# A two-block hybrid model on one core: where early sums, biases, softmax scaling and modulation passes stand around the first output projection

## The chip, the cores and the metric

The kernel runs as one program on one core of a Trainium2 chip. The metric is the device time of one execution in microseconds. Three runs of the kernel before gave a median of 2509.61 us (2504.63 to 2519.35). A core has TensorE (PE, with its weight loads PEld), VectorE (DVE), ScalarE (ACT), GpSimd (POOL) and SyncE (SP), each with its own instruction stream; they meet at semaphores. SP issues the loads of weights, POOL those of the modulation weights.

## The reference

Two blocks follow each other on x of 256 tokens by 2048. The first is a mixer of attention (8 heads of 128) and a state space part (16 heads of 64) side by side, then a gated FFN with a convolution. What the change touches is the first block's mixer:

```python
mod = jax.nn.silu(c) @ w_ada[l] + b_ada[l]
shift_m, scale_m, gate_m, shift_f, scale_f, gate_f = jnp.split(mod[:, None, :], 6, axis=-1)
h = rms_norm(x, norm_mix_g[l]) * (1.0 + scale_m) + shift_m
proj = h @ w_in[l]
q, k, v, xs, z, bmat, cmat, dt_raw = jnp.split(proj, split_at, axis=-1)
attn = moba_attention(q.reshape(hd), k.reshape(hd), v.reshape(hd), rel_bias)
attn = rms_norm(attn, attn_norm_g[l])
ssm = ssd_mixer(xs, z, bmat, cmat, dt_raw, conv_w, conv_b, dt_bias, a_log, d_skip, norm_g)
mix = jnp.concatenate([attn, ssm], axis=-1) @ w_out[l]
x = x + gate_m * mix
h = rms_norm(x, norm_ffn_g[l]) * (1.0 + scale_f) + shift_f
x = x + gate_f * conv_ffn(h, w_up[l], conv_ffn_w[l], conv_ffn_b[l], w_down[l])
```

With 256 tokens there is one attention block: softmax(q k^T / sqrt(128) + bias by distance, causal) v. In the state space part, with dt = softplus(dt_raw + dt_bias) and cs the running sum of -exp(a_log) dt, head h gives y[l] = sum over s <= l of (C_l . B_s) exp(cs_l - cs_s) dt_s x_s, plus d_skip x, times silu(z), and a norm over each half of the width.

## The kernel before, in words

Everything is held transposed, channels on partitions and the 256 tokens in the free dimension. A weight matrix is streamed in units of 128 x 2048 fp32 (1 MB). SP loads a unit into one of four slots of w_raw (load_w, a slot is reloaded once TensorE has used it), ScalarE casts it to w_hi (`hi`, `hi_unit`), VectorE takes the rest w_lo = w_raw - w_hi (`lo`, `lo_unit`), and TensorE makes three matmuls for each product: hi by hi, hi by lo, lo by hi. h_both holds the normed activations, h_hi and h_lo, in the same split. `chunk` runs four units over four output tiles in four PSUM banks.

The modulation vector is worked out on VectorE beside all this: `ada(pair, slot)` multiplies a load of 128 x 2048 in one of two slots of ada_raw by c and sums it into one column of mod. POOL issues the load of a pair when the pass two before it is done. There are 192 passes in all, 2 x 96; those up to 63 are done before the first output projection, 64 to 79 in it, and each engine's stream is written out by hand, so the place of a pass in VectorE's order is fixed.

The stretch in question, in order:
- the input projection IN1 ends with the tokens' v. VectorE and ScalarE take it out of PSUM, cast and cut units 0 and 1 of OUT1;
- TensorE turns the dt and running-sum rows, makes C B^T and turns x (16 transposes); VectorE masks and makes x_tok in four products;
- SP has written the running sums to DRAM (cs_rows) and, once IN1's last unit is used, spreads them over the partitions into cs_b (four loads, in the place of h_hi). For each of 16 heads ScalarE forms the difference and the exponential in one of four buffers lm (L1314, L1325), VectorE multiplies by the masked C B^T (L1989), TensorE multiplies by x_tok (L549, L550), and VectorE adds it to xbc. Behind heads 2, 6, 10 and 14 stands an ada pass;
- VectorE multiplies by silu(z) (ssm_gated); ScalarE squares it, TensorE sums the squares with a matrix of ones (`stat`, L766);
- attention runs in two halves b of four heads: scores on TensorE, logits with bias on VectorE, exps on ScalarE with the row sums, reciprocals on VectorE, `scaled` (L1342) on ScalarE, transposes on TensorE (L988), `turned` and `attended` copies on ScalarE, the product with v (L994, L995);
- the attention output is squared, summed and normed, and OUT1 (U_OUT1, 16 units; L769 to L771) starts with its two state space units, then takes the two attention units. Its chunks end in add_to_x (L2041);
- mix_sq holds the squares of the first 12 tiles of x, VectorE reduces them to mix_sum (L2142), and with the last four tiles they give the norm ahead of the FFN's first half (UP1A, L774).

The bias tiles are loaded from a DRAM scratch in which POOL's bias row was put; the load of half 0 waits for the last state space output (ssm_y 8), since it lies where dt and lm lie, that of half 1 for ssm_gated 2.

## Time and profile before

| | |
|---|---|
| median of 3 runs | 2509.61 us (2504.63 to 2519.35) |
| profiled execution | 2508.57 us |
| its span in the profile | 2506.9 us |
| TensorE busy | 96% |
| VectorE busy | 75% |
| ScalarE busy | 46% |
| mean DMA rate | 245 GB/s |

The profile is of one execution. Times within it are microseconds from the start of its span. Matmuls are pipelined: the start of one row to the start of the next is what one costs, and the duration in a row overlaps its follower.

### The profile page before, as it was taken

To read this page: it belongs to the slowest core of one execution; us is meant where nothing else is said; L and a number is where in the kernel's file an instruction comes from. 1 tells how busy PE (TensorE), PEld (TensorE's weight loads), DVE (VectorE), ACT (ScalarE), POOL (GpSimd) and SP (SyncE) were. 2 spreads that over 40 slices of the span, in tenths; PEclk is the share of its full clock that TensorE was granted. 3 is DMA by queue.
4 is the path that set the end of the run, shared out by engine and by line. 5 is a ranking of instruction groups with operands and counts; after the bars stand their busy time and mean duration, and the time that the engine had idled before them with its cause. 6 is when DMAs were issued, how large, how long until landed. Compare 5 with 4: busy or idle time off the path is not lost.

```text
span 2506.9 us, 42171 instructions
## 1 busy us (share of the span) xinstructions
PE 2395.3 (96%) x17090; PEld 2130.7 (85%) x17090; DVE 1892.5 (75%) x2272; ACT 1142.3 (46%) x1288; POOL 87.8 (4%) x184
## 2 busy tenths in 40 slices
PE   8999959899999999999899999999999999999998
PEld 6799849888888888888799888888888888888887
DVE  6778879888887788887988677668888655566655
ACT  2144364455654345553544344433655543455442
POOL 0010001000000000000000000000000000000000
PEclk9999979899999999999999999899999999999999
DMA  9988948677787887778577123318776555555552
GB/s 398 420 339 331 339 166 315 259 295 288 269 302 296 336 322 278 277 266 326 224 296 305 69 92 117 106 63 300 270 271 238 187 189 185 185 188 196 186 220 100
DMA packets 88533, 614.75 MB, mean 245 GB/s; under 512 B 9657, under 2 KB 13393, under 8 KB 15057
## 3 DMA queue, kind: packets, MB, share of 16 engines
q1 hardware_dynamic: 65218, 444.03, 47.1%
q0 software_dynamic: 23184, 168.83, 17.8%
q8 instruction: 100, 1.64, 0.3%
q14 instruction: 31, 0.25, 0.0%
HBM read 608.60 MB, written 4.22 MB: 244 GB/s over the span
## 4 chain that ended last, share of the span: by engine, by line
PE 76%; DVE 11%; DMA 8%; ACT 3%; issue 2%; SPq 0%; DVEq 0%; POOLq 0%; ACTq 0%
PE ps L774 37%; PE ps L776 19%; PE ps L769 4%; PE ps L771 4%; PE ps L770 4%; DMA first_raw<-in_ada_stream 4%; DVE ada_raw L1748 2%; DMA ada_raw<-in_ada_stream 2%; DMA w_raw<-in_w_stream 1%; DVE w_lo L1736 1%; DVE w_lo L1732 1%; PE ps L655 1%; ACT w_hi L1174 1%; PE ps L816 1%; DVE xbc L1898 1%
## 5 line engine op out<-in xcount | busy, mean ns | idle before, releaser
L774 PE MATMUL ps<-h_both,w_hi 128*128 128x512 f32 x2816 | 987.1, 395 | 10.2 <-DVE h_both L1773 9.2
L776 PE MATMUL ps<-h_both,w_lo 128*128 128x256 f32 x2816 | 789.2, 280 | 0.0
L774 PEld LDWEIGHTS ps<-h_both,w_hi 128*128 128x128 f32 x2816 | 529.7, 188 | 135.3 <-issue 11.7
L1732 DVE TENSOR_TENSOR w_lo<-w_raw,w_hi 128x2048 fp32r<-128x2048 f32 x217 | 495.2, 2287 | 95.2 <-ACT w_hi L1168 88.1
L776 PEld LDWEIGHTS ps<-h_both,w_lo 128*128 128x128 f32 x2816 | 533.3, 189 | 0.0
L1168 ACT CAST w_hi<-w_raw 128x2048 fp32r<-128x2048 f32 x218 | 415.5, 1911 | 247.5 <-DMA w_raw<-in_w_stream 231.1
L774 PE MATMUL ps<-hid_both,w_hi 128*128 128x512 f32 x1344 | 471.7, 394 | 3.4 <-DVE w_lo L1736 3.4
L769 PE MATMUL ps<-h_both,w_hi 128*128 128x256 f32 x1408 | 406.7, 289 | 23.7 <-DVE h_both L1773 7.4
L1736 DVE TENSOR_TENSOR w_lo<-w_raw,w_hi 128x2048 fp32r<-128x2048 f32 x139 | 317.9, 2289 | 143.0 <-ACT w_hi L1174 140.8
L770 PE MATMUL ps<-h_both,w_hi 128*128 128x256 f32 x1408 | 399.6, 284 | 0.0
L771 PE MATMUL ps<-h_both,w_lo 128*128 128x256 f32 x1408 | 399.5, 284 | 0.0
L1174 ACT CAST w_hi<-w_raw 128x2048 fp32r<-128x2048 f32 x138 | 262.6, 1908 | 281.6 <-DMA w_raw<-in_w_stream 280.0
L1748 DVE SCALAR_TENSOR_TENSOR ada_raw<-ada_raw,ada_c 128x2048 f32<-128x2048 f32 x160 | 365.2, 2284 | 28.5 <-DMA ada_raw<-in_ada_stream 28.4
L776 PE MATMUL ps<-hid_both,w_lo 128*128 128x256 f32 x1344 | 375.1, 279 | 0.0
L774 PEld LDWEIGHTS ps<-hid_both,w_hi 128*128 128x128 f32 x1344 | 251.8, 187 | 64.8 <-issue 4.5
L769 PEld LDWEIGHTS ps<-h_both,w_hi 128*128 128x128 f32 x1408 | 271.2, 193 | 31.9 <-issue 13.0
L770 PEld LDWEIGHTS ps<-h_both,w_hi 128*128 128x128 f32 x1408 | 271.5, 193 | 0.3
L771 PEld LDWEIGHTS ps<-h_both,w_lo 128*128 128x128 f32 x1408 | 271.3, 193 | 0.0
L776 PEld LDWEIGHTS ps<-hid_both,w_lo 128*128 128x128 f32 x1344 | 251.9, 187 | 0.0
L2056 DVE SCALAR_TENSOR_TENSOR conv_y<-tmp,par,conv_y 128x254 f32<-128x254 f32 (+1 forms) x352 | 146.4, 478 | 5.1
L2335 POOL DMA_DIRECT2D ada_raw<-in_ada_stream x160 | 84.6, 529 | 1661.2 <-DVE ada_raw L1748 1628.4
L2049 DVE TENSOR_TENSOR tmp<-ps,tmp 128x1024 f32<-128x1024 f32 x44 | 53.9, 1224 | 113.3 <-ACT tmp L1380 113.3
(359 smaller groups left out, 2017.1 us busy)
## 6 DMA issues: line engine op xcount, KB each, us to landing
w_raw<-in_w_stream SPq DMA_DIRECT2D x364, 1024.0 KB, 4.9
ada_raw<-in_ada_stream POOLq DMA_DIRECT2D x160, 1024.0 KB, 6.5
first_raw<-in_ada_stream SPq DMA_DIRECT2D x32, 1024.0 KB, 12.6
w_more<-in_w_stream SPq DMA_DIRECT2D x8, 1024.0 KB, 14.9
kept_raw<-in_w_stream SPq DMA_DIRECT2D x4, 1024.0 KB, 8.1
x<-in_x_t SPq DMA_DIRECT2D x1, 2048.0 KB, 7.9
cs_b<-cs_rows SPq DMA_DIRECT2D x4, 512.0 KB, 7.5
x_kept<-x SPq DMA_DIRECT2D x1, 2048.0 KB, 14.8
```

The source lines that it names most:

```text
L769: mm(o, hi, r_hi, start=first, stop=False, **kw)
L770: mm(o, hi, r_lo, start=False, stop=False, **kw)
L771: return mm(o, lo, r_hi, start=False, stop=last, **kw)
L774: mm(ps[:, b, :].rearrange("p (a t) -> p a t", a=2), hi, both[:, :, k], start=first, stop=False, skip_group_check=True)
L776: return mm(ps[:, b, T:512], lo, big[:, k], start=False, stop=False, skip_group_check=True)
L1168: nc.scalar.copy(w_hi[:, slot], w_raw[:, slot]).then_inc(hi_ready, 1)
L1174: nc.scalar.copy(w_hi[:, u % 4], w_raw[:, u % 4]).then_inc(hi_ready, 1)
L1732: tt(w_lo[:, slot], w_raw[:, slot], w_hi[:, slot].bitcast(F32), ALU.subtract).then_inc(lo_ready, 1)
L1736: tt(w_lo[:, u % 4], w_raw[:, u % 4], w_hi[:, u % 4].bitcast(F32), ALU.subtract).then_inc(lo_ready, 1)
L1748: stt(out=rows, in0=rows, scalar=1.0, in1=ada_c[:], op0=ALU.mult, op1=ALU.mult, accum_out=col(mod, pair)).then_inc(ada_done, 1)
L2056: last = stt(out=conv_y[:, par_, i, d:T], in0=tmp[:, i, 0:T - d], scalar=pc(par_name, o + 2 - d), in1=conv_y[:, par_, i, d:T], op0=ALU.mul ...
L2335: G.dma_start(ada_raw[:, slot], src).then_inc(ada_loaded[slot], 16)
```

## The change

The cs_b load of the first four heads goes to tmp, and is issued ahead of the end of IN1; the bias tiles lie in tiles 8 to 15 of h_lo and are loaded right behind cs_b. x_tok is made and awaited in two halves. w_lo and w_hi of OUT1's unit 1 are made later, those of units 2 and 3 at other places. `scaled(0)` and `turned(0)` move from ScalarE to VectorE. The PSUM banks of the two halves of attention are exchanged, so that OUT1's first unit can run once half 0 is copied out; the sums for the attention norm come behind that unit. The ada passes 60 to 63 are placed differently, 64 to 75 run ahead of the cuts of chunks 1 to 3 of OUT1, and 76 to 79 behind the last of them. Context lines are cut.

```diff
@@ -209,6 +209,9 @@
             prob_t_a = sb(under, "prob_t", [P, 4, 384])
+        with ExitStack() as under:
+            sb(under, "before_bias", [P, 24, T])
+            bias = [sb(under, f"bias{b}", [P, 4, T]) for b in range(2)]
         h_both = sb(ctx, "h_both", [P, 2, KT, T], F32R)
@@ -243,7 +246,7 @@
                 sb(under, "xbc_heads", [P, HT, T])
-                bias_b = sb(under, "bias_b", [P, 4, T])
+                sb(under, "xbc_pairs", [P, 4, T])
                 logit_b = sb(under, "logit_b", [P, 4, 384])
@@ -253,7 +256,7 @@
             with ExitStack() as t:
-                bias = [sb(t, "bias", [P, 4, T]), bias_b]
+                sb(t, "dt_room", [P, 4, T])
                 logit = [sb(t, "logit", [P, 4, 384]), logit_b]
@@ -460,20 +463,17 @@
+            src = bass.AP(tensor=cs_rows, offset=0, ap=[[0, P], [T, 4], [1, T]])
+            sp.dma_start(tmp[:], src).then_inc(side_loaded[0], 16)
+            sp.wait_ge(bias_built, 1)
+            sp.dma_start(scratch.ap(), bias_row[:]).then_inc(bias_out, 16)
+            sp.wait_ge(bias_out, 16)
             sp.wait_ge(units_used, U_OUT1 + 2)
-            for q in range(4):
+            for q in range(1, 4):
                 src = bass.AP(tensor=cs_rows, offset=4 * q * T, ap=[[0, P], [T, 4], [1, T]])
...
             units(U_OUT1 + 3, U_OUT1 + 4)
-
-            sp.wait_ge(bias_built, 1)
-            sp.dma_start(scratch.ap(), bias_row[:]).then_inc(bias_out, 16)
-            sp.wait_ge(bias_out, 16)
             for b in range(2):
-                if b:
-                    sp.wait_ge(S("ssm_gated"), 2)
-                else:
-                    sp.wait_ge(S("ssm_y"), 8)
                 src = bass.AP(tensor=scratch, offset=b * 4 * 384, ap=[[1, P], [384, 4], [1, T]])
@@ -541,6 +541,8 @@
+            if h % 8 == 0:
+                pe.wait_ge(S("x_tok"), h // 8 + 1)
             pe.wait_ge(S("lm"), h + 1)
@@ -955,12 +957,12 @@
             last.then_inc(S("cb"), 1)
-            for t in range(2):
-                for j in range(8):
-                    last = nc.tensor.transpose(ps[:, 3 + 2 * t + j // 4, (j % 4) * P:(j % 4) * P + P],
-                                               xbc[:, j, t * P:t * P + P], ident[:])
-            last.then_inc(S("x_turned"), 1)
-            pe.wait_ge(S("x_tok"), 1)
+            for f in range(2):
+                for t in range(2):
+                    for j in range(4 * f, 4 * f + 4):
+                        last = nc.tensor.transpose(ps[:, 3 + 2 * t + f, (j % 4) * P:(j % 4) * P + P],
+                                                   xbc[:, j, t * P:t * P + P], ident[:])
+                last.then_inc(S("x_turned"), 1)
             for h in range(SSM_HEADS):
@@ -981,23 +983,25 @@
                 pe.wait_ge(S("probs"), b + 1)
-                if b:
+                if not b:
                     pe.wait_ge(root_ready, 3)
...
                     for j, src in enumerate((256, 0, 128)):
-                        last = nc.tensor.transpose(ps[:, 4 - 4 * b + i, j * P:j * P + P], logit[b][:, i, src:src + P], ident[:])
+                        last = nc.tensor.transpose(ps[:, 4 * b + i, j * P:j * P + P], logit[b][:, i, src:src + P], ident[:])
                 last.then_inc(S("probs_turned"), 1)
...
                 for i in range(4):
-                    h, o = 4 * b + i, 4 - 4 * b + i
+                    h, o = 4 * b + i, 4 * b + i
                     mm(ps[:, o, 0:T], v_tok[:, 0, h * P:h * P + P], prob_t[b][:, i, 0:T], start=True, stop=False)
...
                 last.then_inc(S("pv"), 1)
-            pe.wait_ge(S("att_out"), 2)
-            stat(3, b=7)
+            pe.wait_ge(S("att_out"), 1)
             opens(OUT1)
             for i in range(4):
+                if i == 1:
+                    pe.wait_ge(S("att_out"), 2)
+                    stat(3, b=7)
                 pe.wait_ge(lo_ready, U_OUT1 + i + 1)
@@ -1301,7 +1305,6 @@
             in1_evac(7, 1)
-            hi(0, 1, U_OUT1)
@@ -1310,8 +1313,9 @@
                     act.wait_ge(S("ssm_sums"), h - 3)
+                sums = tmp if h < 4 else cs_b
                 for t in range(2):
-                    last = A(lm[:, h % 4, 256 * t:256 + 128 * t], cs_b[:, h, 128 * t:T], ACT.Relu,
+                    last = A(lm[:, h % 4, 256 * t:256 + 128 * t], sums[:, h, 128 * t:T], ACT.Relu,
                              bias=dt_tok[:, 2 + t, h:h + 1], scale=-1.0)
@@ -1326,6 +1330,8 @@
                 stat(1 + g, [xbc[:, 4 * g + k] for k in range(4)], N_H1 + 16)
+                if not g:
+                    hi(0, 1, U_OUT1)
@@ -1345,22 +1351,22 @@
                 act.wait_ge(S("probs_turned"), b + 1)
-                nc.scalar.copy(prob_t[b][:], ps[:, 4 - 4 * b:8 - 4 * b, 0:384]).then_inc(S("prob_t"), 1)
+                act.wait_ge(S("prob_t"), b)
+                nc.scalar.copy(prob_t[b][:], ps[:, 4 * b:4 * b + 4, 0:384]).then_inc(S("prob_t"), 1)
...
                 act.wait_ge(S("pv"), b + 1)
-                nc.scalar.copy(qk[:, 4 * b:4 * b + 4], ps[:, 4 - 4 * b:8 - 4 * b, 0:T]).then_inc(S("att_out"), 1)
+                nc.scalar.copy(qk[:, 4 * b:4 * b + 4], ps[:, 4 * b:4 * b + 4, 0:T]).then_inc(S("att_out"), 1)
...
             exps(0)
-            exps(1)
             act.wait_ge(sq_used, sq_base[3])
...
                 bank_root(1 + g, 512, bank(0, T * g, T * g + T))
+            exps(1)
             for g in range(2):
                 power(1 + g)
-            scaled(0)
+            act.wait_ge(S("probs"), 1)
             scaled(1)
-            turned(0)
             norm(N_SSM, HT, zero[:4])
@@ -1368,6 +1374,7 @@
             stat(3, [qk[:, k] for k in range(HT)], N_ATT)
+            hi(0, 2, U_OUT1)
             bank_root(3, WIDTH, bank(7))
@@ -1437,7 +1444,6 @@
-            hi(0, 2, U_OUT1)
             hi(0, 3, U_OUT1)
@@ -1957,7 +1963,6 @@
             in1_evac(7, 1)
-            lo(0, 1, U_OUT1)
@@ -1967,14 +1972,14 @@
                 steps.add(tt(cb_t[:, g, T:384], ps[:, 1 + g, T:384], tri[:, 0:P], ALU.mult))
-            dve.wait_ge(S("x_turned"), 1)
             dve.wait_ge(S("dt_tok"), 1)
-            for t in range(2):
-                for f in range(2):
+            for f in range(2):
+                dve.wait_ge(S("x_turned"), f + 1)
+                for t in range(2):
                     last = tt(x_tok[:, t, 512 * f:512 * f + 512].rearrange("p (h v) -> p h v", h=8),
...
                               dt_tok[:, t, 8 * f:8 * f + 8].unsqueeze(2).to_broadcast([P, 8, 64]), ALU.mult)
-            last.then_inc(S("x_tok"), 1)
+                last.then_inc(S("x_tok"), 1)
@@ -2018,20 +2023,38 @@
+            def scaled(b):
+                dve.wait_ge(S("att_r"), b + 1)
+                for q, (o, n) in enumerate(((0, T), (T, P))):
+                    for i in range(4):
+                        last = ts(logit[b][:, i, o:o + n], logit[b][:, i, o:o + n], att_r[b][:, 4 * q + i:4 * q + i + 1],
+                                  None, ALU.mult)
+                last.then_inc(S("probs"), 1)
+
+            def turned(b):
+                dve.wait_ge(S("probs_turned"), b + 1)
+                V.tensor_copy(prob_t[b][:], ps[:, 4 * b:4 * b + 4, 0:384]).then_inc(S("prob_t"), 1)
+
             logits(0)
             logits(1)
-            next_ada()
             inverse_sums(0)
-            next_ada()
+            scaled(0)
             inverse_sums(1)
+            lo(0, 1, U_OUT1)
+            turned(0)
             inverse(1)
...
             next_ada(2)
+            lo(0, 2, U_OUT1)
+            next_ada()
+            inverse(3)
+            for k in (0, 4):
+                norm(N_ATT + k, 3, [qk[:, k + j] for j in range(4)], [pcol("attn_g", k + j) for j in range(4)], zero, k)
+            lo(0, 3, U_OUT1)
+            next_ada()
             assert pair == 64
-            inverse(3)
-            norm(N_ATT, 3, [qk[:, k] for k in range(HT)], [pcol("attn_g", k) for k in range(HT)], zero, 0)
@@ -2136,7 +2159,24 @@
             mod_bias(GATE_M, KT)
-            stream(U_OUT1, OUT1, 0, 4, add_to_x(U_OUT1, GATE_M), 64, 4)
+            added = add_to_x(U_OUT1, GATE_M)[0]
+            ada(64, 0)
+            lo(1, 0, U_OUT1)
+            ada(65, 1)
+            lo(1, 1, U_OUT1)
+            added(0, OUT1 % 2)
+            ada(66, 0)
+            lo(1, 2, U_OUT1)
+            ada(67, 1)
+            lo(1, 3, U_OUT1)
+            for c in (2, 3):
+                for i in range(4):
+                    ada(4 * c + (60 + i), i % 2)
+                    lo(c, i, U_OUT1)
+                    if i == 1:
+                        added(c - 1, (OUT1 + c - 1) % 2)
+            for q in range(76, 80):
+                ada(q, q % 2)
             lo_unit(U_UP1A)
...
             V.tensor_reduce(mix_sum[:], mix_sq[:].rearrange("p k t -> p t k"), AX_X, ALU.add).then_inc(S("mix_sum"), 1)
```

## Rows read from the trace of the kernel before

**Rows 1.** The page: span, busy time and share of each engine

```profile
span 2506.9 us, 42171 instructions
...
PE 2395.3 (96%) x17090; PEld 2130.7 (85%) x17090; DVE 1892.5 (75%) x2272; ACT 1142.3 (46%) x1288; POOL 87.8 (4%) x184
```

**Rows 2.** Timeline, PE: start us, us, line, operation, count, idle before and releaser

```profile
366.50 2.79 PE L988 MATMUL ps<-ident,logit 128*128 128x128 f32 x12 [12.14 <-ACT logit L1342]
...
369.92 1.53 PE L988 MATMUL ps<-ident,logit_b 128*128 128x128 f32 x12 [0.62 <-ACT logit_b L1342]
...
378.70 3.69 PE L766 MATMUL ps<-tmp,ones 128*128 128x256 f32 x16 [1.64 <-ACT tmp L1185]
...
382.04 0.47 PE L769 MATMUL ps<-h_both,w_hi 128*128 128x256 f32 x1
...
385.10 0.28 PE L769 MATMUL ps<-h_both,w_hi 128*128 128x256 f32 x1
...
385.22 0.28 PE L770 MATMUL ps<-h_both,w_hi 128*128 128x256 f32 x1
...
396.82 0.55 PE L769 MATMUL ps<-h_both,w_hi 128*128 128x256 f32 x1 [2.93 <-DVE w_lo L1732]
...
479.96 0.70 PE L1012 MATMUL ps<-mix_sum,ones 128*128 128x256 f32 x2 [0.75 <-DVE mix_sum L2142]
```

**Rows 3.** Timeline, DVE, end of the first output projection

```profile
465.46 2.29 DVE L1732 TENSOR_TENSOR w_lo<-w_raw,w_hi 128x2048 fp32r<-128x2048 f32 x1 [0.33 <-ACT w_hi L1168]
...
467.80 2.29 DVE L1748 SCALAR_TENSOR_TENSOR ada_raw<-ada_raw,ada_c 128x2048 f32<-128x2048 f32 x1
...
472.04 2.29 DVE L1736 TENSOR_TENSOR w_lo<-w_raw,w_hi 128x2048 fp32r<-128x2048 f32 x1 [1.94 <-ACT w_hi L1168]
...
474.25 5.66 DVE L2142 TENSOR_REDUCE mix_sum<-mix_sq 128x256 f32<-128x3072 f32 x1
...
479.82 1.65 DVE L2041 SCALAR_TENSOR_TENSOR x<-ps,mod,x 128x256 f32<-128x256 f32 x4
```

**Rows 4.** Timeline, ACT, from the decays to attention

```profile
317.00 1.49 ACT L1314 ACTIVATE lm<-cs_b,dt_tok 128x256 f32<-128x256 f32 x4 [2.66 <-DMA cs_b<-cs_rows]
...
349.95 1.63 ACT L1185 ACTIVATE tmp<-xbc 128x256 f32<-128x256 f32 x4 [3.25 <-PE ps L766]
...
357.91 0.51 ACT L1334 ACTIVATE logit_b<-logit_b,att_m 128x256 f32<-128x256 f32 x1 [0.55 <-DVE att_m L2015]
...
361.43 0.81 ACT L1200 ACTIVATE rstd<-ps,eps 128x256 f32<-128x256 f32 x2
...
366.25 3.61 ACT L1342 ACTIVATE logit_b<-logit_b,par,att_r 128x256 f32<-128x256 f32 x8
...
377.09 1.01 ACT L1352 COPY qk<-ps 128x1024 f32<-128x1024 f32 x1 [0.31 <-PE ps L995]
```

**Rows 5.** Timeline, DVE, heads and first logits

```profile
313.07 2.29 DVE L1732 TENSOR_TENSOR w_lo<-w_raw,w_hi 128x2048 fp32r<-128x2048 f32 x1 [1.72 <-ACT w_hi L1168]
...
316.47 2.47 DVE L1974 TENSOR_TENSOR x_tok<-ps,dt_tok 128x512 f32<-128x512 f32 x4
...
327.27 0.56 DVE L1989 TENSOR_TENSOR lm<-lm,cb_t 128x384 f32<-128x384 f32 x1 [0.76 <-ACT lm L1325]
...
349.45 0.42 DVE L2007 SCALAR_TENSOR_TENSOR logit<-ps,bias 128x256 f32<-128x256 f32 x1 [2.98 <-DMA bias<-bias_rows]
```

**Rows 6.** Windows: PE, PEld, DVE, ACT, POOL busy, granted clock, DMA share, GB/s

```profile
360.00:370.00 10.00, 2.87 (x13) 2.50 (x14) 4.15 (x10) 10.00 (x29) 1.06 (x2) 0.52 0.56 210
```

**Rows 7.** Tile ada_raw, the two loads issued at 465.8 and 470.8 us

```profile
L2335 POOL DMA_DIRECT2D ada_raw<-in_ada_stream x1: 527/527/527, 465.8 to 465.8; - x1
...
DMA to landing us min/median/max: 7.8/7.8/7.8
...
L2335 POOL DMA_DIRECT2D ada_raw<-in_ada_stream x1: 527/527/527, 470.7 to 470.7; - x1
...
DMA to landing us min/median/max: 9.0/9.0/9.0
```

## The prediction

> **What bounds it now.** I read the page first: TensorE is busy 96% of the span [rows 1], so the whole is a row of projections that TensorE paces, and a change to the stage between two of them is worth what it does to the moments at which TensorE starts on one and leaves the next. The diff touches three stretches: the state space heads and attention, the first output projection (OUT1, 16 units), and the hand-over from OUT1 to the first half of the FFN. So I read TensorE's timeline there [rows 2]. OUT1 begins at 382.04. Its matmuls follow each other every 0.12 us, so one unit (48 of them) takes 5.76 us and 16 take 92.2. It ends at 479.2 (the row of 479.96 less its idle 0.75), 97.2 us later: 92.2, plus the wait of 2.93 before unit 2 for its low half, plus some 1.5 of matmuls at a lower clock behind that wait (0.55 us for the first, 0.28 for those at 385), plus 0.5 of seams. Then the chain of waits goes through VectorE: TensorE waits 0.75 for mix_sum, and the last addition to x starts at 479.82 [rows 3]. So two sums are wanted: how much earlier TensorE ends OUT1, and how much later than that end VectorE starts the last addition. Everything behind it has the same order in both kernels and moves with it one to one.
>
> **Part 1, the heads (early sums, halves of x_tok, one cut of w_lo moved away).** ScalarE's first decay waited 2.66 us for cs_b and began at 317.00 [rows 4]. VectorE cut w_lo from 313.07, 2.29 us, before it could read the turned dt, then came the mask and four x_tok products of 2.47, to 318.94 [rows 5]. The cut and its cast (1.9) leave this place, so VectorE reaches its first head at about 317.0: -2.0. The sums of heads 0 to 3 now come into tmp, issued behind the third OUT1 unit some five us before the old place, so they should lie there when the decays start at about 312.5, behind the table load. ScalarE then fills all four lm buffers before VectorE needs the first. In the trace the product of head 6 begins at 327.27, 8.3 us behind the end of x_tok; VectorE's own work between is six such products, one ada pass and two y additions, about 6.0 us, and some 0.6 of waiting for TensorE's heads will be left. I take -1.7 for the whole and 0 to -2.5 as bounds; later groups were paced by a loop over the three engines that does not change. **SP's queue** has the cost: the bias rows' write and the wait for its completion now stand ahead of cs_b 1 to 3. If that write lands 3 us late, head 4's decay starts near 319, when VectorE is in its ada pass, so it costs nothing. Unit 3 and both bias loads come next on SP, and SP's next work waits for TensorE's first OUT1 unit anyway. Heads: -3.7.
>
> **Part 2, the biases.** VectorE waited 2.98 us for the bias load [rows 5], which itself waited for the last y. In tiles 8 to 15 of h_lo they land some 20 us before use: -3.0. Logits start at 349.45 - 3.7 - 3.0 = 342.8. What is late next is ScalarE: its second four squares (349.95, 1.63 us, paced by TensorE's sums behind the scores [rows 4]) move by 3.7 alone and end at 347.9, against 347.0 for the logits (4.2 us a half). The cast moved between the squares (1.91) falls into a wait of 3.25 in the same row, so it costs nothing.
>
> **Part 3, softmax on two engines.** ScalarE: exps(0) 347.9 plus 3.52 (from 357.91 to 361.43 [rows 4]) = 351.4; two logarithms 0.75; exps(1) to 355.7; powers to 356.3; scaled(1) 3.6 (the row of 366.25) to 359.9, against 369.86 before: one scaling of 3.5 gone, the rest from the earlier start. VectorE's scaled(0) is not in this trace. Its nearest rows are the logit operations, 0.42 each with 0.28 for the narrow ones: eight in 2.1 to 2.8 us; half of that if it runs faster on SBUF. Taken 2.1, it ends at 353.9; it is covered by exps(1), and the cover is still there at 2.8. VectorE then waits for exps(1), cuts w_lo (0,1) to 358.2 and copies prob_t (0) from PSUM, 1.4 to 2.0, to 359.9. TensorE turns half 1 at about 360, so this copy hides too, by 1.5 us. The new wait of ScalarE's copy on VectorE's costs nothing. TensorE: the second transposes took 1.53 and the first 2.79 at the lower clock [rows 2], granted 0.52 there [rows 6]; the two products with v ran from 371.3 to 376.8. 359.9 + 1.5 + 5.8, and 1.3 for the clock, is 368.5.
>
> **Part 4, the projection behind half of attention.** Before, TensorE stood between 376.8 and 382.04 for the copy of half 1 (1.02 [rows 4]), the squares, and their sums (3.69 [rows 2]). Now unit 0 lies there, 368.5 to 374.3; sums to 378.0; unit 1 to 383.8. OUT1 starts 13.5 earlier, but the sums stand inside it (-9.8 net). Unit 2 needs the first four attention tiles and w_lo (0,2). ScalarE casts that unit before it takes the root: 376.4 to 378.3; VectorE cuts to 380.5, makes one ada pass (2.29) to 382.8, and then four tiles and their low halves (3.3): 386.1. TensorE waits 2.3 us and loses 1.5 to the clock, as in the row of 396.82; unit 3 starts when w_lo (0,3) is cut, about 393, and ends at 399.2. In the trace this end is 479.2 - 69.1 = 410.1. VectorE has one ada, one bias sum, one ada and the cut of (1,0) between: 399.4, so TensorE waits 0.2. The twelve units left take 69.1 if weights arrive: **OUT1 ends at 468.6, that is -10.6.** Bounds: -7 (no early sums, longer first wait) to -13 (no wait before unit 2).
>
> **Part 5, the ada passes at the end.** The count before the last addition is the same, their places are not: four are run behind the last cut of OUT1 (pairs 76 to 79), and only one was. Their slots are two, and a load is issued when the pass two before is done. Relative to TensorE's end E = 479.2: the cut (3,3) ends at E - 11.4, the one ada pass behind it runs at E - 11.4 to -9.2, then a cut, and mix_sum, 5.66 us, from 474.25 [rows 3]. The loads issued at 465.8 and 470.8 took 7.8 and 9.0 us to land [rows 7]. With the same landings: pass 76 ends at E - 9.2; pass 77 has its data at E - 5.6, ends at -3.3; pass 78 has its data at E + 0.6, ends at +2.8; pass 79's load is issued at E - 2.6 and with some 7 us lands at +4.4, ends at +6.6; cut to +8.8; mix_sum to +14.5. The last addition starts at E + 14.5 and not at E + 0.6: **+13.9**. By VectorE's work alone, no landing waited for, it is three passes of 2.21 less the idle 1.94 [rows 3]: +4.7, the floor. For the loads the Trainium skill ("DMA: Bandwidth & Descriptors", Anatomy of one DMA) gives 2.0 us plus the bytes at 436 GB/s, an estimate of 4.4 us for one of these: the last addition would come at E + 8.3, a part of +7.7 and a total of 2505.5 instead of the one below. The rows have nearly twice that landing time, with weight loads in flight beside them, and the measurement decides.
>
> **Sum.** -10.6 + 13.9 = +3.3. The profiled execution took 2508.57 us, 1.7 over its span of 2506.9 and 1.0 below the median of 2509.61: **2511.9 us**. What the front wins, the ada passes at the hand-over give back.
>
> **Rivals.**
> (a) The loads at the end land sooner, in 5 to 6 us, since fewer lie queued when OUT1 starts earlier with its weights waiting. Then part 5 is +8 to +10 and the total 2506 to 2508. For: nothing saturates the queue at the restart of the new OUT1. Against: in OUT1 one weight unit and one ada load are asked for each 5.8 us in both kernels.
> (b) The passes hide: VectorE is far enough ahead that mix_sum is ready when TensorE ends. Then the head's gain stays, less the floor at most: 2498 to 2503. Against: the cut (3,3) waits for its weights, which wait for TensorE, so VectorE can't be ahead of it [rows 3].
> (c) Slower: in the new order an ada pass stands before the cut of its unit and not behind it. A slot takes landing + 0.7 + 2.3 us for one of two passes; with the 9.0 of [rows 7] that is 6.0 us a unit against TensorE's 5.76, and each unit of chunks 1 to 3 waits 0.24: +3, and +3 to +4 more for the first of them, 2518. It decides from a landing of 8.5 us on; at 10 us it would be +9 and the total 2524.
> (d) The early part does not work as said: tmp's load lies behind a weight unit, the bias write's completion behind both, and head 0 or 4 waits. It costs the 3.7 of part 1: 2515.6.
>
> **Chances.** Forecast 0.50 (2507 to 2516 with its bounds), (a) 0.20, (b) 0.10, (c) 0.10, (d) 0.10. For 8 in 10 the range reaches from 2501 to 2519. A measurement of this kernel can tell about 0.5% (12.5 us) from no change; faster by more than that needs (b) and every bound of the front at its best: 0.06. Slower by more needs (c) at 10 us: 0.06. Within: 0.88.
>
> **What would show it.** Early part: decays from about 312.5, no wait of VectorE for the bias, OUT1's first matmul at 367 to 370, the sums of squares between its first two units, the end of OUT1 at 466 to 471. Late part: four ada passes behind the last cut, waits of VectorE for ada data among them, mix_sum 8 to 14 us after TensorE's last matmul, and TensorE's wait for mix_sum grown from 0.75 us to that. If that wait stays under 3 us, part 5 is wrong and the kernel is faster by 8 to 10 us. If OUT1 ends later than 473, parts 1 to 4 are.

## The result and the profile after

| | before | after |
|---|---|---|
| median | 2510.82 us (2503.31 to 2525.39, 20 runs) | 2522.22 us (2510.76 to 2530.88, 20 runs) |
| ratio, 95% interval | | 1.0041 (1.0029 to 1.0053), or +10.3 us (7.3 to 13.3) |
| profiled execution, its span | 2508.57, 2506.9 us | 2520.63, 2519.0 us |
| granted clock, mean | 0.982 | 0.981 |

The forecast was 2511.9 us, +3.3, with a range that ended at 2519. The change costs 10.3 us. That is within the 0.5% named there, as forecast, but the time lies above the range. The page of after:

```profile
span 2519.0 us, 42172 instructions
PE 2401.2 (95%) x17090; PEld 2134.5 (85%) x17090; DVE 1896.2 (75%) x2281; ACT 1138.1 (45%) x1279; POOL 87.8 (3%) x184
```

The page doesn't say where the time goes: TensorE's busy time is 5.9 us up on before [rows 1], and its idle time 6.2. The stretch that the change touches does. From ScalarE's last copy of v to the FFN's first matmul it lasted 180.90 us before and 189.96 after, with TensorE busy for 141.67 and 141.25 us of it. So there the time is lost between matmuls, not in them, and the 5.9 us lie in later stages, whose order is the same. First the early part. TensorE's timeline of after, from the transposes to the first units of OUT1 (start, us, engine, line, operation, count, idle before and releaser); it answers to [rows 2]:

```profile
355.23 2.79 PE L990 MATMUL ps<-ident,logit 128*128 128x128 f32 x12 [3.87 <-DVE logit L2030]
361.32 2.23 PE L990 MATMUL ps<-ident,logit_b 128*128 128x128 f32 x12 [3.31 <-ACT logit_b L1348]
...
369.52 0.36 PE L771 MATMUL ps<-h_both,w_hi 128*128 128x256 f32 x1
...
375.35 3.62 PE L768 MATMUL ps<-tmp,ones 128*128 128x256 f32 x16
...
387.34 0.36 PE L771 MATMUL ps<-h_both,w_hi 128*128 128x256 f32 x1 [2.62 <-DVE h_both L1779]
...
393.64 0.39 PE L771 MATMUL ps<-h_both,w_hi 128*128 128x256 f32 x1 [0.31 <-DVE w_lo L1738]
...
400.67 0.36 PE L771 MATMUL ps<-h_both,w_hi 128*128 128x256 f32 x1 [1.02 <-DVE w_lo L1738]
```

OUT1 begins at 369.52, one unit runs, the sums of squares stand behind it at 375.35, and three short waits follow. All of this is as forecast, to about a microsecond. Now the hand-over, VectorE's timeline of after, which answers to [rows 3]:

```profile
458.99 2.28 DVE L1738 TENSOR_TENSOR w_lo<-w_raw,w_hi 128x2048 fp32r<-128x2048 f32 x1
461.96 2.29 DVE L1754 SCALAR_TENSOR_TENSOR ada_raw<-ada_raw,ada_c 128x2048 f32<-128x2048 f32 x1 [0.68 <-DMA ada_raw<-in_ada_stream]
...
468.30 2.29 DVE L1754 SCALAR_TENSOR_TENSOR ada_raw<-ada_raw,ada_c 128x2048 f32<-128x2048 f32 x1 [4.05 <-DMA ada_raw<-in_ada_stream]
...
473.48 2.29 DVE L1754 SCALAR_TENSOR_TENSOR ada_raw<-ada_raw,ada_c 128x2048 f32<-128x2048 f32 x1 [2.87 <-DMA ada_raw<-in_ada_stream]
...
479.85 2.29 DVE L1754 SCALAR_TENSOR_TENSOR ada_raw<-ada_raw,ada_c 128x2048 f32<-128x2048 f32 x1 [4.07 <-DMA ada_raw<-in_ada_stream]
...
482.06 2.29 DVE L1742 TENSOR_TENSOR w_lo<-w_raw,w_hi 128x2048 fp32r<-128x2048 f32 x1
484.27 5.29 DVE L2182 TENSOR_REDUCE mix_sum<-mix_sq 128x256 f32<-128x3072 f32 x1
489.48 1.65 DVE L2064 SCALAR_TENSOR_TENSOR x<-ps,mod,x 128x256 f32<-128x256 f32 x4
```

The cut of unit (3,3) starts at 458.99. Behind it stand four ada passes, and each waits for its data, 11.67 us in all. Only then come a cut, mix_sum and the last addition, at 489.48. TensorE's row at that place:

```profile
489.61 1.22 PE L1016 MATMUL ps<-mix_sum,ones 128*128 128x256 f32 x2 [19.61 <-DVE mix_sum L2182]
```

It has been idle for 19.61 us, against 0.75 before [rows 2]: its last matmul of OUT1 ends at 470.0. The addition was at 479.82 before [rows 3], so the stretch is 9.66 us longer, and the FFN's first matmul moves by the same (491.55 to 501.21). Behind it the order is the same in both kernels. The two profiled executions differ by 12.1 us at the end, and the 2.4 us beyond the 9.7 have no one place: table loads of the later stages that answer to each other lie 9.5 us apart at 504 us, 14.6 at 1271, 9.2 at 1964 and 12.1 at the end. The ratio's +10.3 (7.3 to 13.3) agrees with the 9.7 of the stretch.

### The profile page after: what moved, and what is told of

The parts are those of the page before. It is cut to its first block, busy times and chain, and to the rows that moved or that the text cites. A ratio compares the mean times of both kernels' runs of the same rounds, so it can differ in the third digit from the quotient of the medians.

```text
span 2519.0 us, 42172 instructions
## 1 busy us (share of the span) xinstructions
PE 2401.2 (95%) x17090; PEld 2134.5 (85%) x17090; DVE 1896.2 (75%) x2281; ACT 1138.1 (45%) x1279; POOL 87.8 (3%) x184
## 4 chain that ended last, share of the span: by engine, by line
PE 74%; DVE 11%; DMA 9%; ACT 3%; issue 2%; SPq 0%; POOLq 0%; DVEq 0%; ACTq 0%
PE ps L776 37%; PE ps L778 19%; PE ps L771 4%; DMA first_raw<-in_ada_stream 4%; PE ps L772 4%; PE ps L773 4%; DMA ada_raw<-in_ada_stream 3%; DVE ada_raw L1754 2%; DVE w_lo L1742 1%; DMA w_raw<-in_w_stream 1%; DVE w_lo L1738 1%; PE ps L657 1%; ACT w_hi L1178 1%; DVE xbc L1904 1%; PE ps L683 1%
## 6 DMA issues: line engine op xcount, KB each, us to landing
first_raw<-in_ada_stream SPq DMA_DIRECT2D x32, 1024.0 KB, 12.6
```

## Experiments

Each stage is measured in the same way in every kernel. S is the start of ScalarE's last copy of v, ahead of all that the change touches (310.65 before, 311.25 after). P is the first matmul of OUT1, E the end of its last (the start of the mix_sum matmul less its idle time), A the start of the last addition to x. All are starts in the timelines, in us.

| kernel | P - S | E - P | E - S | A - E | A - S | ratio to before (95%) |
|---|---|---|---|---|---|---|
| before | 71.39 | 97.17 | 168.56 | 0.61 | 169.17 | 1 |
| after | 58.27 | 100.48 | 158.75 | 19.48 | 178.23 | 1.0041 (1.0029 to 1.0053) |
| before_late_passes | 70.32 | 92.49 | 162.81 | 18.88 | 181.69 | 1.0044 (1.0029 to 1.006) |
| half_ada_loads | 60.54 | 101.72 | 162.26 | 10.43 | 172.69 | 0.9991 (0.9974 to 1.0008) |
| tail_behind_add | 56.55 | 102.49 | 159.04 | -0.05 | 158.99 | 1.0006 (0.9993 to 1.002) |
| two_passes_earlier | 59.19 | 103.30 | 162.49 | 8.02 | 170.51 | 1.0015 (0.9999 to 1.0032) |
| earlier_and_behind | 57.62 | 103.07 | 160.69 | 0.36 | 161.05 | 0.9968 (0.9952 to 0.9985) |
| eb_norm_first | 59.54 | 106.06 | 165.60 | 1.17 | 166.77 | 0.9995 (0.9983 to 1.0007) |
| eb_sums_first | 62.94 | 94.27 | 157.21 | 0.41 | 157.62 | 0.9967 (0.9951 to 0.9984) |
| eb_bias_late | 61.44 | 102.67 | 164.11 | 0.21 | 164.32 | 0.998 (0.9965 to 0.9995) |
| sums_first | 62.45 | 93.46 | 155.91 | 18.88 | 174.79 | 1.0029 (1.0011 to 1.0047) |
| eb_sums_late | 61.31 | 101.43 | 162.74 | 0.93 | 163.67 | 0.9989 (0.9976 to 1.0002) |
| es_scaled_on_act | 69.26 | 93.86 | 163.12 | 0.20 | 163.32 | 0.998 (0.9966 to 0.9994) |
| best_cuts_first | 63.44 | 92.77 | 156.21 | 1.14 | 157.35 | 0.9971 (0.996 to 0.9983) |

One caution. After, half_ada_loads and tail_behind_add have the same order of work up to P, and their P - S are 58.27, 60.54 and 56.55. A figure that rests on P - S carries 2 us either way, and E - S differs by 1.8 us between two_passes_earlier and earlier_and_behind, whose order up to E is the same; A - E is steadier (18.88, 18.88 and 19.48 in the three kernels with four late passes). A ratio's interval is 3 to 4.5 us to either side. Each verdict below rests on both, or says on which.

### The late passes alone, on the kernel before

```diff
-            stream(U_OUT1, OUT1, 0, 4, add_to_x(U_OUT1, GATE_M), 64, 4)
+            added = add_to_x(U_OUT1, GATE_M)[0]
+            lo(0, 2, U_OUT1)
+            lo(0, 3, U_OUT1)
+            ada(64, 0)
+            lo(1, 0, U_OUT1)
...
+            for q in range(76, 80):
+                ada(q, q % 2)
```

> The kernel before, with nothing of the front of the change; only the ada passes of OUT1 stand as in the changed kernel: the cuts of units 2 and 3 come first, then each pass ahead of the cut of its unit, and 76 to 79 behind the last cut. Theory (place of the passes is the loss): OUT1 ends some 4 us earlier than in the kernel before (no 2.9 us wait, no slow matmuls behind it), near 475, and the last addition starts 18 to 20 us behind it, near 494: +14 us, 2524. Rival (the end is set by TensorE and a fixed amount of VectorE work): +4.7 behind the end, the last addition near 480, 2510.

Measured: 2524.68 us, ratio 1.0044. Of the whole change only the placement of the passes in OUT1 was taken over, with the cuts of units 2 and 3 ahead of them, and the loss is there in full:

```profile
483.26 2.29 DVE L1748 SCALAR_TENSOR_TENSOR ada_raw<-ada_raw,ada_c 128x2048 f32<-128x2048 f32 x1 [3.69 <-DMA ada_raw<-in_ada_stream]
...
487.68 5.29 DVE L2161 TENSOR_REDUCE mix_sum<-mix_sq 128x256 f32<-128x3072 f32 x1
...
493.02 1.22 PE L1012 MATMUL ps<-mix_sum,ones 128*128 128x256 f32 x2 [19.01 <-DVE mix_sum L2161]
```

Pass 79 waits 3.69 us for its load and starts 9.2 us behind E; TensorE idles 19.01 us. Here E - P is 92.49 against 97.17, and TensorE's timeline has no wait between its first matmul of OUT1 and this one, since the low halves of units 2 and 3 no longer stand behind passes. A - S rises by 12.5 us, the ratio by 11.0.

### The same passes with shorter loads

```diff
+                G.dma_start(ada_raw[:, pair % 2, 0:D // 2], a["ada_stream"][pair][:, 0:D // 2])
```

This for pairs 64 to 79 of after; so these loads bring half of each row and the modulation from them isn't the reference's. VectorE's instructions are the same.

> The changed kernel, whose ada loads 64 to 79 bring only half of each row, so that mod comes out wrong in those columns; VectorE's passes are as long as before. Theory (the passes at the end wait for landings): their waits of 4.1, 2.9 and 4.1 us go, four passes of 2.2, a cut and mix_sum of 5.3 run back to back behind the cut of (3,3): the last addition starts 7 to 8 us behind the end of OUT1 instead of 19.5, about -12 against the changed kernel, 2510. Rival (VectorE's own work and order is what is late, landings are incidental): less than 3 us gained.

Measured: 2511.27 us, ratio 0.9991. A - E falls from 19.48 to 10.43 with not one instruction of VectorE taken out, so 9 us of it is the landing of loads. It did not fall to the 7 or 8 us that were expected. The half loads issued around the end of OUT1 still took 4.3 to 6.9 us to land, and the last pass still waited:

```profile
474.17 2.29 DVE L1754 SCALAR_TENSOR_TENSOR ada_raw<-ada_raw,ada_c 128x2048 f32<-128x2048 f32 x1 [2.98 <-DMA ada_raw<-in_ada_stream]
...
DMA to landing us min/median/max: 4.3/5.5/6.9
```

The whole is less clear than A - E. The profiled execution, at 2516.78 us, is the slowest of the ten, and its E - S is 3.5 us longer than after's, so its A - S is only 5.5 us below after's, where the ratios say 12.6. The record has no place for that difference.

### The four passes behind the last addition

```diff
-            for q in range(76, 80):
-                ada(q, q % 2)
...
             add_to_x(U_OUT1, GATE_M)[0](3, (OUT1 + 3) % 2)
+            for q in range(76, 80):
+                ada(q, q % 2)
```

> The changed kernel with passes 76 to 79 moved behind the last addition to x, ahead of gains_of. Theory: the last addition starts 6 us behind the end of OUT1 (cut and mix_sum of 5.3 first), near 476 and not 489.5; the passes then take the time of squares, sums and root, but the load of pass 79 starts only when pass 77 is done, so the norm ahead of UP1A starts near 490 instead of 497.8: -8 us, 2514. Rival (the chain of passes and landings is what sets the norm wherever it stands): the norm starts where it does now, within 2 us.

Measured: 2513.74 us, ratio 1.0006. The addition starts at E - 0.05, earlier than the E + 6 expected, since mix_sum is ready when TensorE ends. But the passes make the scale and shift that the next norm needs, so they only moved to the next wait:

```profile
468.91 1.66 DVE L2064 SCALAR_TENSOR_TENSOR x<-ps,mod,x 128x256 f32<-128x256 f32 x4
470.48 2.28 DVE L1754 SCALAR_TENSOR_TENSOR ada_raw<-ada_raw,ada_c 128x2048 f32<-128x2048 f32 x1
...
478.47 2.29 DVE L1754 SCALAR_TENSOR_TENSOR ada_raw<-ada_raw,ada_c 128x2048 f32<-128x2048 f32 x1 [3.49 <-DMA ada_raw<-in_ada_stream]
...
486.35 1.67 DVE L1775 SCALAR_TENSOR_TENSOR tmp<-x,gain,rstd 128x256 f32<-128x256 f32 x4
```

TensorE, which has waited for its squares, waits 15.28 us more for the normed tiles. The norm starts at 486.35, against 497.80 in after; measured from S, the FFN's first matmul is 10.1 us earlier than there, and the ratios say 8.8. So half of what the addition gained was kept.

### Two passes earlier, and two passes earlier with two behind

VectorE waits twice in the attention stage of after, 2.06 us for exps(1) and 4.79 for the cast of unit 2. Two passes go into these waits, the cut of unit 1 goes behind the norms of the state space half, and only two passes are left behind the last cut of OUT1. In the second kernel these two stand behind the last addition.

```diff
             scaled(0)
+            next_ada()
             inverse_sums(1)
-            lo(0, 1, U_OUT1)
+            next_ada()
             turned(0)
...
+            lo(0, 1, U_OUT1)
             next_ada(2)
...
-            for q in range(76, 80):
+            for q in range(78, 80):
```

> The changed kernel with two ada passes in VectorE's waits inside attention (behind scaled(0) and behind the second reciprocal), the cut (0,1) behind the norms of the state space half, and every later pass two places earlier, so that two and not four stand behind the last cut. Theory: each place is worth a landing cycle of about 5.7 us; the last pass ends 11 us sooner, the last addition starts near 478 to 479, OUT1's end stays at 470: -11 against the changed kernel, 2511. Rival (work alone): two passes of 2.2 us fewer, -4.4.

> The changed kernel with both cures: the later passes two places earlier, as in two_passes_earlier, and the last two (78, 79) behind the last addition. Theory: nothing of the passes stands ahead of mix_sum, and their landings lie behind squares and sums: the last addition starts within 1 us of the end of OUT1 (473), the norm ahead of UP1A starts near 481 to 482 against 488.15 in the kernel before and 497.8 in the changed one: 2503 to 2505, faster than both. Rival (the two cures take the same time away twice): as two_passes_earlier, 2511 to 2514.

Measured: 2513.83 us, ratio 1.0015, for two passes earlier; 2503.23 us, ratio 0.9968, with the other two behind the addition. A - E is 8.02 in the first and 0.36 in the second, whose TensorE row is:

```profile
470.99 0.70 PE L1016 MATMUL ps<-mix_sum,ones 128*128 128x256 f32 x2 [0.49 <-DVE mix_sum L2173]
```

The norm now starts at 479.66, and from the addition to the FFN's first matmul it takes 12.2 us against 11.73 before, so the two passes lie almost wholly in waits that were there. The second kernel keeps the gain of the early part: A - S is 8.1 us below before's, and the ratio says -8.0. The first was expected at 2511 and came 3 us later, since E - S was 3.7 us more than in after; the second, with the same early order, has 1.9 us of that. A part may be the spread named above, and a part the price of the passes' new places: unit 2 waits 3.63 and 3.73 us in these two kernels, and 2.62 in after. No run separates the two.

### The norm ahead of a pass

In earlier_and_behind, unit 2 waits 3.73 us for the normed attention tiles, and VectorE's norm stands behind a pass that itself waited 1.02 us for its load. The obvious mend is to move that pass behind the cut of unit 3:

```diff
             lo(0, 2, U_OUT1)
-            next_ada()
             inverse(3)
...
             lo(0, 3, U_OUT1)
-            next_ada()
+            next_ada(2)
```

> earlier_and_behind with pass 64 moved from between the cut (0,2) and the attention norm to behind the cut (0,3). Theory: unit 2 of OUT1 waited 3.6 us for the norm, of which this pass and its landing were 3.2; the wait shrinks to under 1, but the cut (1,0) then stands behind two passes: OUT1 ends 2 to 3 us earlier than in earlier_and_behind, and the total follows, 2501 to 2502. Rival (the landings of the passes set the end of the stage, not TensorE): unchanged within 1 us.

Measured: 2508.98 us, ratio 0.9995, so some 6 us slower and not 1 to 2 faster. The wait at unit 2 went (3.73 to 0.40), and a longer one came in its place:

```profile
399.92 2.29 DVE L1754 SCALAR_TENSOR_TENSOR ada_raw<-ada_raw,ada_c 128x2048 f32<-128x2048 f32 x1 [3.44 <-DMA ada_raw<-in_ada_stream]
402.13 2.28 DVE L1738 TENSOR_TENSOR w_lo<-w_raw,w_hi 128x2048 fp32r<-128x2048 f32 x1
...
404.68 0.55 PE L771 MATMUL ps<-h_both,w_hi 128*128 128x256 f32 x1 [6.65 <-DVE w_lo L1738]
```

The load of pass 66 can only be issued when pass 64 is done, and that pass now ran at 391.88, in its parent at 380.74. It was issued at 394.8, landed 5.0 us later, and the cut that TensorE needs stood behind it. This is the mechanism of rival (c), a pass ahead of a cut that a late load holds up, in a place where it shows plainly. By the stage the move costs 4.9 us (E - S), by the ratios 6.8.

### The projection begun behind half of attention, or not

```diff
-            pe.wait_ge(S("att_out"), 1)
+            pe.wait_ge(S("att_out"), 2)
+            stat(3, b=7)
             opens(OUT1)
             for i in range(4):
-                if i == 1:
-                    pe.wait_ge(S("att_out"), 2)
-                    stat(3, b=7)
```

This was made on earlier_and_behind and on after.

> earlier_and_behind with the projection no longer begun behind half of attention: TensorE waits for both halves and makes the sums of squares before unit 0. Theory: OUT1's first matmul comes 5.5 us later (about 375.5), but the root and the attention norm come earlier by that too, so unit 2 no longer waits and OUT1 ends where it did within 2 us: the begun projection is worth little. Rival (the early unit is worth its length, as the sum of the prediction has it): OUT1's end and the total +5.8.

> The changed kernel, its ada passes untouched, with TensorE making the sums of squares of both halves before unit 0 of OUT1. Theory (in the changed kernel the end of the stage hangs on the chain of passes and landings, which starts from what VectorE does, not on TensorE): OUT1 ends some 3 to 4 us earlier, as it did when this was done to earlier_and_behind, and the last addition moves by less than half of that; the gap between the two grows from 19.5 to 21 or more; total within 2 us of the changed kernel's 2522. Rival (the addition follows TensorE's end at a fixed distance): the addition and the total -3.5.

Measured: eb_sums_first 2500.74 us, ratio 0.9967; sums_first 2514.83 us, ratio 1.0029. OUT1 begins 5.3 and 4.2 us later, and ends 3.5 and 2.8 us earlier, measured from S. The sums come first and the norm is done by the time unit 2 wants it:

```profile
370.40 3.69 PE L768 MATMUL ps<-tmp,ones 128*128 128x256 f32 x16 [1.64 <-ACT tmp L1187]
...
468.56 0.70 PE L1014 MATMUL ps<-mix_sum,ones 128*128 128x256 f32 x2 [0.55 <-DVE mix_sum L2171]
```

E - P is 94.27, near the 92.2 of 16 units, where earlier_and_behind has 103.07. So the unit that is begun early buys nothing: it holds the sums back by its 5.8 us, and root, norm and unit 2 come that much later. The stage shows this in both pairs, by somewhat more than the 1.8 us by which E - S differs without a cause; the ratios don't contradict it but can't show it alone (0.9967 against 0.9968, 1.0029 against 1.0041, the intervals overlap). In sums_first A - E stays at 18.88: the addition followed the earlier end of OUT1, which I had not expected, since I took the chain of loads to run on its own clock. My reading is that VectorE's order ties the passes to the units: each stands behind a cut, which waits for its cast and so for a slot that TensorE frees. No run takes that tie away.

### The biases and the early sums, one at a time

```diff
             for b in range(2):
+                if b:
+                    sp.wait_ge(S("ssm_gated"), 2)
+                else:
+                    sp.wait_ge(S("ssm_y"), 8)
```

```diff
-            sp.dma_start(tmp[:], src).then_inc(side_loaded[0], 16)
...
-            for q in range(1, 4):
+            for q in range(4):
...
-                sums = tmp if h < 4 else cs_b
+                sums = cs_b
```

Both were made on earlier_and_behind, the one where a gain of the early part reaches the end.

> earlier_and_behind with the bias loads again behind the last state space output. Theory: VectorE waits about 3 us again, of which ScalarE's squares had covered 1.3, so TensorE's products and OUT1 move by 1.7 and the total by 1.5 to 2. Rival: the whole 3.0; or nothing, if the end of the stage hangs on the passes and not on attention.

> earlier_and_behind with the running sums of the first four heads again in cs_b, loaded only once the input projection is done. Theory: ScalarE's first decay starts near 317 instead of 314.5, the heads lose 1.5 to 2.5 us and OUT1's first matmul and end move by as much. Rival: nothing, since VectorE has x_tok to make until 317.4 anyway.

Measured: eb_bias_late 2508.31 us, ratio 0.998; eb_sums_late 2505.77 us, ratio 0.9989. The two waits are back where they were:

```profile
349.33 0.42 DVE L2016 SCALAR_TENSOR_TENSOR logit<-ps,bias 128x256 f32<-128x256 f32 x1 [3.38 <-DMA bias<-bias_rows]
```

```profile
318.51 1.49 ACT L1316 ACTIVATE lm<-cs_b,dt_tok 128x256 f32<-128x256 f32 x4 [5.40 <-DMA cs_b<-cs_rows]
```

The first is VectorE's row of eb_bias_late, the second ScalarE's of eb_sums_late. E - S is 3.4 and 2.05 us more than with both, the ratios say 3.0 and 5 us; the expectation was 1.7 to 2 for the bias and 1.5 to 2.5 for the sums. Both edits do what they say, as the waits show. What each is worth is less sure: by the stage 3.4 and 2 us, with the spread named above on each, both profiled executions were the slowest of their ten, and the intervals of the ratios overlap the parent's.

### The scaling on ScalarE again

```diff
             for g in range(2):
                 power(1 + g)
-            act.wait_ge(S("probs"), 1)
+            scaled(0)
             scaled(1)
+            turned(0)
```

Made on eb_sums_first, with scaled(0) and turned(0) taken from VectorE.

> eb_sums_first (2500.7) with softmax scaling and the first copy of half 0 back on ScalarE. Theory: ScalarE's chain of exps, powers and scaling is what TensorE waits for, so the 3.5 us of scaling(0) come back, less up to 1.5 since TensorE turns half 0 meanwhile at a higher clock: OUT1's first matmul +2 to +3.5, total 2503 to 2504. Rival: nothing, VectorE's placed passes hide it.

```profile
363.97 2.79 PE L990 MATMUL ps<-ident,logit 128*128 128x128 f32 x12 [10.02 <-ACT logit L1346]
```

Measured: 2503.51 us, ratio 0.998, 3.3 us more than the parent; E - S is 5.9 more, over the 2 to 3.5 expected. The first exponentials began 2.5 us later here for a reason ahead of the edit (40.11 behind S, against 37.56), which is the spread again. From there to scaled(1) it took 11.83 us and not 8.62, so 3.2 us are the scaling's own, and that agrees with the ratio. The edit also takes `turned(0)` back to ScalarE, so scaling and copy are tested together.

### The version that beats both

```diff
                 for i in range(4):
-                    ada(4 * c + (62 + i), i % 2)
                     lo(c, i, U_OUT1)
                     if i == 1:
                         added(c - 1, (OUT1 + c - 1) % 2)
+                    ada(4 * c + (62 + i), i % 2)
```

Made on eb_sums_first: in chunks 1 to 3 the cut that TensorE needs comes first and the pass behind it.

> eb_sums_first with each cut of chunks 1 to 3 ahead of its ada pass and not behind it. Theory: the wait of 1.0 us of TensorE for the cut (1,0) goes, OUT1 takes 93.3 instead of 94.3 us, and nothing else changes, as the landings are as long: -1, 2499.7, which only the trace can tell. Rival: passes that stand ahead of cuts keep the loads going; behind them they start later, and pass 78 or 79 delays the norm.

Measured: 2500.76 us (2497.08 to 2503.45), ratio 0.9971 (0.996 to 0.9983), 7.3 us under the kernel before. E - P is 92.77, 0.6 over 16 units back to back, so the wait for the cut (1,0) went as expected. But TensorE waits 1.27 us for mix_sum, 0.55 in the parent, and A - S is only 0.3 us less. The 1 us expected on the whole isn't shown: earlier_and_behind, eb_sums_first and this kernel have ratios of 0.9968, 0.9967 and 0.9971, which their intervals can't tell apart. It keeps all early edits of the change but the projection begun behind half, and puts two passes in attention's waits and two behind the last addition.

## Why the prediction was right and wrong

**Part 1, the heads: right.** The decays were forecast at 312.5 and began at 314.51, since S itself came 0.6 us later and ScalarE then waited 1.38 us for tmp's load; VectorE's first product with a head was forecast at 317.0 and came at 317.43. For the heads as a whole -3.7 was taken; the first product with z comes 4.1 us earlier relative to S. The bias write on SP's queue cost nothing that shows; rival (d) fell.

**Part 2, the biases: right.** Logits forecast at 342.8, measured 342.90 with no wait. Late next were ScalarE's squares, as said: exps(0) follows them at once at 349.33, forecast 347.9.

**Part 3, softmax on two engines: right.** The rows of after:

```profile
353.20 1.92 DVE L2030 TENSOR_SCALAR logit<-logit,att_r 128x256 f32<-128x256 f32 x8
...
359.46 1.75 DVE L2036 COPY prob_t<-ps 128x1536 f32<-128x1536 f32 x1
```

```profile
357.67 3.60 ACT L1348 ACTIVATE logit_b<-logit_b,par,att_r 128x256 f32<-128x256 f32 x8
```

Scaling on VectorE 1.92 us (taken 2.1, bounds 1.05 to 2.8), the copy 1.75 (1.4 to 2.0), scaled(1) at 357.67 (356.3). OUT1's first matmul was forecast at 368.5 and came at 369.52.

**Part 4, the projection behind half: right in its size, wrong as a gain.** Unit 1 started at 378.62 (forecast 378.0), unit 2 at 387.34 behind a wait of 2.62 (386.1, 2.3), unit 3 waited 0.31, unit (1,0) 1.02 (0.2). OUT1 ended at 470.0, that is -9.2 and not -10.6, within the bounds; 1.0 us of that was there at the first matmul. What the working did not ask is whether the sums could have stood first: the two runs with them first end OUT1 another 2.8 and 3.5 us earlier. The "-9.8 net" of that part counted the early start and not what it put behind the norm.

**Part 5, the ada passes at the end: the mechanism right, the size off.** This is the step that failed. The addition was forecast at E + 14.5 and came at E + 19.5, so the term is +18.9 and not +13.9. The path through it is pass 75, whose end lets the load of 77 be issued, pass 77, the load of 79, pass 79, a cut, mix_sum:
- 3.1 us lie ahead of it. The working took the end of the cut (3,3) and of the passes around it from before, and so had pass 75 done at E - 14.1 (pass 77's data at E - 5.6, less 7.8 and 0.7). It was done at E - 11.0. In the new order a pass stands ahead of each cut, and in chunks 1 to 3 of OUT1 seven of them waited for their loads, 0.29 to 1.87 us each.
- 2.4 us are landings. I took 7.8 us for the load of 77 and 7 for that of 79, the latter below both loads of [rows 7] and without a reason; they took 8.6 each.
- mix_sum took 5.2 us and not 5.66, which gives 0.4 back.

For the 3.1 us the waits are borne out as the cause by half_ada_loads, which has the same order: passes 66 to 75 waited 0.7 us in all there and 5.9 in after, and pass 75 was done at E - 14.6. Its row in after, then in half_ada_loads (E is 470.00 and 473.37):

```profile
456.77 2.29 DVE L1754 SCALAR_TENSOR_TENSOR ada_raw<-ada_raw,ada_c 128x2048 f32<-128x2048 f32 x1 [1.42 <-DMA ada_raw<-in_ada_stream]
```

```profile
456.60 2.28 DVE L1754 SCALAR_TENSOR_TENSOR ada_raw<-ada_raw,ada_c 128x2048 f32<-128x2048 f32 x1
```

The landings of after:

```profile
L2375 POOL DMA_DIRECT2D ada_raw<-in_ada_stream x3: 528/530/530, 459.7 to 471.3; - x3
...
DMA to landing us min/median/max: 8.5/8.6/8.6
```

The window beside it shows why a price for a quiet queue is no price here (busy time of PE, PEld, DVE, ACT and POOL, granted clock, DMA share, GB/s):

```profile
460.00:470.00 10.00, 10.00 (x84) 9.80 (x82) 5.27 (x4) 3.81 (x2) 0.79 (x2) 1.00 0.96 370
470.00:480.00 10.00, 0.01 (x1) 0.00 (x0) 3.06 (x5) 0.00 (x0) 1.05 (x2) 0.73 0.87 324
```

The DMA engines are busy 96% and 87% of the two stretches. SP issues three weight units of the same size between 458 and 471, and these took 7.2 to 8.4 us to land. The Trainium skill ("DMA: Bandwidth & Descriptors", Anatomy of one DMA) gives an estimate of 4.4 us for such a load; the trace doesn't agree, with 8.6 us for loads that have weight loads beside them. The prediction's total by that estimate has a small slip: its own terms, -10.6 and +7.7, make 2505.7 and not 2505.5. In eb_norm_first a load issued at 394.8 landed in 5.0 us, 0.6 over the estimate. The six microseconds ahead of it had a DMA share of 0.46, its own flight one of 0.94; so the share during the flight doesn't set the landing alone, and what was queued ahead is the likely difference, which no run isolates.

**The sum.** -9.2 + 18.9 = +9.7, forecast -10.6 + 13.9 = +3.3. Of the 6.4 us, 1.4 lie ahead of E (1.0 of them in parts 1 to 3, with the 0.6 us by which S came later) and 5.0 are part 5's. Measured on the whole: +10.3. The 6.4 alone would have put the time at 2518.3, just inside the range. The rest of the way to 2522.2 is 2.2 us by which the median of before, 2510.82, lies above the one execution of 2508.57 us that the forecast was added to, and 1.7 us without a place, within the interval of the ratio.

**The rivals.** (a), sooner landings, fell: they were later. (b), passes that hide, fell: TensorE waited 19.61 us. (d) fell. Of (c) the mechanism was there and its price sat elsewhere. With landings of 8.5 to 9 us the passes ahead of the cuts did wait, but VectorE was far enough ahead that TensorE did not stall in each unit; instead the waits delayed the chain at the end by the 3.1 us above. TensorE did wait for the first of them, 1.02 us, where (c) had 3 to 4. Forecast and (c) were written as cases that exclude each other, and they added. The range took each alone. That the forecast's upper bound of 2516 and the 6 us of (c) make the measured 2522 is chance: the prices sat elsewhere.

## What to carry to other kernels

A step with a distant deadline, whose load waits for the buffer of the step two before, is a chain: with two slots each pass at the end cost (8.6 landing + 0.7 to the issue + 2.2 work) / 2, some 5.75 us, where its work alone is 2.2. In this kernel such steps did best in waits that the engine has anyway, and behind the work that TensorE waits for, and if one is moved, the loads of those behind it move too (eb_norm_first: 6.65 us of TensorE for a pass moved behind one cut). A large stage begun early is no gain by itself: ask what the early piece pushes behind itself, and price a load by a row with the same streams beside it.

## What the runs showed of the hardware

- Landing of a 1 MB load by POOL's queue, from its issue: 8.5 to 8.6 us at the end of OUT1 in after, with the DMA engines busy for 87 to 96% of the time; 5.0 us in eb_norm_first, in a stretch at 94% that followed one at 46%. Half of the bytes took 4.3 to 6.9 us, with a median of 5.5, at a share of 0.85 to 0.90 (half_ada_loads).
- Eight scalings by a column in fp32, from SBUF to SBUF, took VectorE 1.92 us from the first start to the last end. The single rows last 0.35 us for 256 columns and 0.28 for 128 at the longest and shortest, and overlap. The Trainium skill ("VectorE: DVE Perf Modes", The perf-mode tier table) has such operations at twice the rate of those with two tensors. The slope agrees: 0.075 us for 128 columns more, against 0.14 in the logit operations of after (0.42 and 0.28, two tensors, one in PSUM). But what doesn't depend on the columns is so large that for 128 columns nothing is left of it, 0.28 us either way.
- TensorE's granted clock in after was 1.00 in 460 to 470, a mean of 0.73 in 470 to 480, where TensorE was idle, and 0.50, the level of 1.2 GHz, in 480 to 490. The two matmuls with mix_sum, at 489.61, took 1.22 us and not 0.70. This cost nothing that shows: from the addition to the FFN's first matmul both kernels took 11.73 us, since ScalarE and VectorE set the pace there (in after TensorE waits 2.22 us for ScalarE's squares and 4.39 for VectorE's tiles).
- The same order of work up to OUT1 took from 56.55 to 60.54 us in three executions. A forecast of single microseconds for a stage can't be tested by one profile.
